# A transformer kernel: stage ends by halves of the tokens, the next stage opened with two natural weight units

## The chip, the cores and the metric

One core of one Trainium2 chip runs the whole program. The metric is the device time in microseconds (us); the median of three runs stands for a kernel. Engines are named as in the profile: PE is TensorE (matmuls, with its weight loads as PEld), DVE is VectorE, ACT is ScalarE, POOL is GpSimd, SP is SyncE, whose queue issues the loads of weights.

## The reference

Batch 1, 256 tokens, model width 1024, float32. Three blocks follow each other: a layer with mixer AB and a dense FFN, one with mixer CD and experts, and a second kind of block. The weight queue moves 475 MB:

```python
for layer in range(DEPTH):        # first_block: layer 0 and layer 1
    mix = _mixer_ab(x, ...) if layer % 2 == 0 else _mixer_cd(x, ...)
    x = _layernorm(ALPHA * x + mix, ln_g[layer, 0], ln_b[layer, 0])
    ffn = _swiglu(x, w1, w3, w2) if layer % 2 == 0 else _moe(x, w_router, w1, w3, w2)
    x = _layernorm(ALPHA * x + ffn, ln_g[layer, 1], ln_b[layer, 1])
# second_block
u = rms_norm(h, mix_norm_g); proj = u @ w_in     # block attention and a convolution
h = h + mixed @ w_out
u = rms_norm(h, ffn_norm_g)
h = h + (silu(u @ w_gate) * (u @ w_up)) @ w_down
return rms_norm(h, final_norm_g)
```

`_mixer_ab` holds gated linear attention and an attention over chosen keys, `_mixer_cd` an attention with forget gates (heads "c") and a dilated one (heads "d"), `_moe` the two best of eight experts.

## The kernel before

**Weights.** Each weight unit is 128 x 2048 float32 values (1 MB). SP loads units in the order in which they are used into a ring of six. Every product keeps float32 accuracy by three products of fp32r halves: ACT copies a unit's upper half (`upper`, line 1270), DVE subtracts it from the unit to give the lower half (`lower`, line 1697), and PE adds high x high, high x low and low x high (`thirds`, lines 611 to 614). There are two pairs of buffers for the halves (`Split.place`), a third one in the expert loop. `split_used` tells ACT that a pair is free, `taken` tells PE and SP that a unit is split. At the ends of stages POOL makes one lower half (its own `lower`, line 2302), at 18 and 18 + 33 units and at the second FFN's first unit.

**Tokens.** The 256 tokens are two tiles of 128 rows, tile 0 and tile 1, in `x[:, t, :]`. For the next stage they are transposed into `xTh` and `xTl`, the halves of x transposed, 8 blocks k of 128 model columns each.

**A stage's end.** The out units (or the last `down` units of an FFN) add up four banks, tile t and column half n in bank 4 + 2t + n. In the last unit, PE goes through (t, n) in the order 00, 01, 10, 11, and each finished bank raises `sums_part` or `sums_done`. DVE adds the residual (`residual_half`, line 1721); ACT computes mean and squared deviations of a tile (`deviations`, lines 1372 to 1374); POOL gives the reciprocal root (`rstd_tiles`, line 2293); DVE centres the tile (line 1756) and norms it by halves (line 1761; in the RMS norm line 1794), which raises `x_half` for tile 0 and `x_ready` for tile 1. PE's `transposes(src, n, spins=...)` (line 690) waits for these and writes banks 0 to 3; around it `keep_busy` issues matmuls on a constant tile (line 605), 16, 5 and 2 of them. ACT then copies four banks to `xTh` (line 1276) and DVE subtracts them to `xTl` (line 1707); `need(k)` in the first product of the next stage waits for `tr_low`.

**Where it happens.** A: end of mixer AB, next the dense FFN. B: end of the dense FFN, next mixer CD. C: end of mixer CD, next the router. D: end of the second block's mixer, next its FFN. The FFNs run chunks of 256 hidden columns: `up` multiplies two units with the weights stationary and both halves of x moving (512 columns, line 841, and 256 for the lower half, line 843), ACT and DVE compute the gate (`silus`, `gates`), and `down` adds the chunk to the sums. Mixer CD starts with `narrow` (forget logits, 8 columns, then a transposition by way of ACT), units in the order q, k, v for each pair of heads, and `cd_gap(i)`, which issues scores, turns and values of the 16 groups in the gaps between and in the middle of units, by hand-written lists (`CD_SCORES` and so on). The scores wait for `forget_low`, written by DVE (line 2051), and for the log-sigmoid (`ls_b`).

Each engine executes its own instruction stream in the order of the program, and they meet only through the semaphores named here.

## Time and profile before

| | |
|---|---|
| median of 3 runs | 1795.53 us (1792.7 to 1796.86) |
| the profiled execution | 1793.35 us, its span 1791.5 us |
| granted clock of PE, mean | 0.997 of 2.4 GHz |
| busy: PE, weight loads, DVE, ACT, POOL | 98%, 83%, 76%, 64%, 9% of the span |
| stages: AB, dense FFN, CD, router, experts, second mixer, second FFN | begin at about 0, 160, 354, 490, 512, 1449, 1591 us |

In the rows below, times are in us from the start of the span, a row's second number is the duration, and brackets hold the idle time of the engine before it and what ended it. `out<-in` names the tiles; for aliased buffers the name can be another tile's at the same place. The durations of matmuls in a row overlap, as PE is pipelined: what counts is the distance of their starts.

### The profile page before, as it was taken

Reading aid. Unit: us, or ns where it says so; the run is one execution under the profiler, and the core shown is the slowest. Engines: PE = TensorE matmul, PEld = TensorE weight load, DVE = VectorE, ACT = ScalarE, POOL = GpSimd, SP = SyncE. Lnnn points to the kernel's source line nnn. Section 1 sums busy time; section 2 is a strip of 40 time slices with the busy share of each in tenths; the row PEclk is TensorE's granted clock in tenths of the full one; section 3 lists DMA queues with packets and bytes.
Section 4 is the critical chain, followed back from the end, with each engine's and each line's share of the span. In section 5 each row is a group of like instructions: output and inputs, shape, how many; then the busy total and the mean of one; then the engine's idle time right before and its main releaser. Section 6 shows DMA issues by size and latency. Waiting matters only on the chain.

```text
span 1791.5 us, 24813 instructions
## 1 busy us (share of the span) xinstructions
PE 1762.9 (98%) x9332; PEld 1479.8 (83%) x9332; DVE 1353.4 (76%) x1280; ACT 1143.5 (64%) x1160; POOL 157.8 (9%) x107
## 2 busy tenths in 40 slices
PE   9999999999999999999999999999999999899998
PEld 7898888889878888888888888888888879878886
DVE  3765655545488888898888888988888888865555
ACT  5655545555467777777777777777777774555443
POOL 0002000100141000000000000000000105510000
PEclk9999999999999999999999999999999999999999
DMA  9845555543489999999999999999999986435550
GB/s 291 272 141 172 188 187 187 176 153 118 155 288 376 389 369 393 358 382 391 349 393 376 364 394 359 379 392 349 394 380 360 396 293 198 140 133 188 189 187 29
DMA packets 260196, 502.86 MB, mean 281 GB/s; under 512 B 15068, under 2 KB 101653, under 8 KB 259758
## 3 DMA queue, kind: packets, MB, share of 16 engines
q1 hardware_dynamic: 252160, 474.67, 74.0%
q0 software_dynamic: 7072, 26.69, 4.8%
q10 hardware_dynamic: 910, 0.76, 0.1%
q8 instruction: 36, 0.59, 0.1%
q14 instruction: 18, 0.15, 0.0%
HBM read 494.18 MB, written 12.65 MB: 283 GB/s over the span
## 4 chain that ended last, share of the span: by engine, by line
PE 89%; DVE 5%; ACT 2%; POOL 2%; DMA 1%; issue 1%; ACTq 0%; DVEq 0%; POOLq 0%; SPq 0%
PE psum L611 23%; PE psum L613 23%; PE psum L614 23%; PE psum L841 9%; PE psum L843 5%; DVE psum L2217 2%; PE psum L1126 1%; DMA ring<-in_w_in 1%; ACT wh L1270 1%; PE psum L750 1%; POOL wl L2302 1%; PE psum L718 1%; DVE x L1761 1%; POOL rstd L2293 1%; PE psum L734 0%
## 5 line engine op out<-in xcount | busy, mean ns | idle before, releaser
L1697 DVE TENSOR_TENSOR wl<-ring,wh 128x2048 fp32r<-128x2048 f32 x437 | 1001.4, 2292 | 248.0 <-ACT wh L1270 245.8
L1270 ACT ACTIVATE wh<-ring 128x2048 fp32r<-128x2048 f32 x450 | 862.3, 1916 | 271.2 <-PE psum L611 169.3
L611 PE MATMUL psum<-wh,xT 128*128 128x512 f32 (+1 forms) x1136 | 431.3, 380 | 1.4 <-DVE xT L1853 1.1
L614 PE MATMUL psum<-wh,xT 128*128 128x512 f32 (+1 forms) x1136 | 424.4, 374 | 0.0
L613 PE MATMUL psum<-wl,xT 128*128 128x512 f32 (+1 forms) x1136 | 424.3, 374 | 0.0
L611 PE MATMUL psum<-wh,wnh 128*128 128x512 f32 x672 | 266.3, 396 | 0.5 <-DVE wnl L1853 0.5
L614 PE MATMUL psum<-wh,wnl 128*128 128x512 f32 x672 | 263.5, 392 | 0.0
L613 PE MATMUL psum<-wl,wnh 128*128 128x512 f32 x672 | 263.5, 392 | 0.0
L841 PE MATMUL psum<-xT,wh 128*128 128x512 f32 x704 | 249.5, 399 | 0.4 <-DVE xT L1707 0.4
L611 PEld LDWEIGHTS psum<-wh,xT 128*128 128x128 f32 x1136 | 214.2, 189 | 43.0 <-issue 3.0
L614 PEld LDWEIGHTS psum<-wh,xT 128*128 128x128 f32 x1136 | 214.0, 188 | 39.8
L613 PEld LDWEIGHTS psum<-wl,xT 128*128 128x128 f32 x1136 | 214.3, 189 | 36.9
L843 PE MATMUL psum<-xT,wl 128*128 128x256 f32 x704 | 197.7, 281 | 0.0
L841 PEld LDWEIGHTS psum<-xT,wh 128*128 128x128 f32 x704 | 132.3, 188 | 33.9 <-issue 1.2
L611 PEld LDWEIGHTS psum<-wh,wnh 128*128 128x128 f32 x672 | 126.3, 188 | 28.4 <-issue 1.4
L614 PEld LDWEIGHTS psum<-wh,wnl 128*128 128x128 f32 x672 | 126.2, 188 | 28.4
L613 PEld LDWEIGHTS psum<-wl,wnh 128*128 128x128 f32 x672 | 126.3, 188 | 25.8
L843 PEld LDWEIGHTS psum<-xT,wl 128*128 128x128 f32 x704 | 132.9, 189 | 0.7
L611 PE MATMUL psum<-xT,wh 128*128 128x256 f32 x384 | 111.0, 289 | 1.9 <-DVE wl L1697 1.7
L613 PE MATMUL psum<-xT,wh 128*128 128x256 f32 x384 | 108.6, 283 | 0.0
L614 PE MATMUL psum<-xT,wl 128*128 128x256 f32 x384 | 108.5, 282 | 0.0
L611 PEld LDWEIGHTS psum<-xT,wh 128*128 128x128 f32 x384 | 73.4, 191 | 4.1 <-issue 3.0
(303 smaller groups left out, 1417.9 us busy)
## 6 DMA issues: line engine op xcount, KB each, us to landing
ring<-in_w_moe SPq DMA_DIRECT2D x336, 1024.0 KB, 6.8
ring<-in_w_dense SPq DMA_DIRECT2D x33, 1024.0 KB, 5.0
ring<-in_w_in_ab SPq DMA_DIRECT2D x14, 1024.0 KB, 10.9
ring<-in_w_in_cd SPq DMA_DIRECT2D x12, 1024.0 KB, 5.2
ring<-in_w_gate SPq DMA_DIRECT2D x11, 1024.0 KB, 5.1
ring<-in_w_up SPq DMA_DIRECT2D x11, 1024.0 KB, 5.2
ring<-in_w_down SPq DMA_DIRECT2D x11, 1024.0 KB, 4.8
ring<-in_w_in SPq DMA_DIRECT2D x6, 1024.0 KB, 8.2
```

Source lines behind the costliest of these rows:

```text
L611: last = pe.matmul(o, a[0], b_[0], start=first, stop=False)
L613: pe.matmul(o, a[0], b_[1], start=False, stop=False)
L614: return pe.matmul(o, a[1], b_[0], start=False, stop=final)
L718: last = pe.matmul(o, q[rows, hp, t * P:(t + 1) * P], k[rows, hp, 0:n], start=True, stop=not (forget or masked))
L750: last = pe.matmul(to[:, o:o + HD], pT[:, g % 2, (2 * hh + s) * P:(2 * hh + s + 1) * P], v[:, s, h * HD:(h + 1) * HD], start=(s == 0), sto ...
L841: first_of(pe.matmul(ps.rearrange("p (a t) -> p a t", a=2), h_[:, k, m], xT_both[:, :, k, :], start=k == 0, stop=False))
L843: last = pe.matmul(ps[:, 0:T], l_[:, k, m], xTh[:, k, :], start=False, stop=k == KT - 1)
L1126: last = pe.transpose(bank[2 + c % 2][:, f * P:(f + 1) * P], mg[:, f * P:(f + 1) * P], ident[:, :])
L1270: act.activation(upper_half[i], ring[:, u_, :], ACT.Copy).then_inc(hi_ready[s_], 1)
L1697: dve.tensor_tensor(lower_half[i], ring[:, u_, :], upper_half[i].bitcast(F32), ALU.subtract)\
L1761: dve.scalar_tensor_tensor(x[:, t, s_], src[:, t, s_], rstd[:, t:t + 1], w[:, 1, s_], ALU.mult, ALU.add).then_inc(x_ready if t else x_half, 1)
L2217: last = dve.scalar_tensor_tensor(summed(c, j), upad[:, c, j:j + T], cw[:, c, j:j + 1], summed(c, j - 1), ALU.mult, ALU.add)
```

## The change

- **Order of the sums.** `out_last` takes the place of the last two out units, `down_last` that of the last two `down` units: tile 0 of both units first, then tile 1.
- **Norms by tile.** `tile_norms` norms tile 0 by halves, its mean and variance from `bn_stats` on DVE; the residuals of tile 1 come behind the first half of tile 0. ACT still makes the deviations of tile 1 (`second_deviations`). `rms_norm` has the same order at D.
- **Pieces.** x is transposed in four pieces (tile, half of the k blocks), each copied and subtracted by itself (`turn_piece`, `copy_piece`, `lower_piece`). Not at C, where only the counts of spins change.
- **The pair.** `tile_pair` opens the dense FFN, mixer CD and the second FFN with two units in natural form (tokens stationary, 256 weight columns moving): the products with the upper weight halves piece by piece, then those with the lower halves. In the FFNs the pair is the first chunk's w1 and w3; its gate is computed in natural form on ACT and DVE (`silu_pair`, `gate_pair`) and transposed (`turn_hidden`); `first_up` takes the upper halves of the next unit first. In mixer CD the pair is the values of heads c, so q and k come after, and the lists of gaps move.
- **Buffers.** The third pair of halves, whose space is tq, nr, pr and pT, is used in the FFNs and for the units at their ends as well. POOL no longer makes lower halves at A, B and D; DVE makes them.

The diff, cut:

```diff
-CD_SCORES = [0, 1, 2, 3, 4, 5, 6, 7, 10, 11, 12, 13, 16, 17, 18, 19]
-CD_TURNED = [2, 3, 4, 5, 6, 7, 8, 9, 12, 13, 14, 15, 17, 18, 19, 20]
-CD_VALUES = [3, 4, 5, 6, 7, 8, 9, 10, 13, 14, 15, 16, 18, 19, 20, 21]
-CD_OUT_TURNED = [8, 14, 20, 22]
+CD_SCORES = [2, 3, 4, 5, 6, 7, 8, 9, 11, 12, 13, 14, 16, 17, 18, 19]
+CD_TURNED = [4, 5, 6, 7, 8, 9, 10, 11, 13, 14, 15, 15, 17, 18, 19, 20]
+CD_VALUES = [5, 6, 7, 8, 9, 10, 11, 12, 14, 15, 16, 16, 18, 19, 20, 21]
+CD_OUT_TURNED = [10, 15, 20, 22]
...
             AB["ra"], AB["ra"] + 256, AB["qb"] + 256, AB["kb"] + 256, AB["vb"] + 256]
-CD_ORDER = [CD[n + h] + 256 * i for h in "cd" for i in range(2) for n in "qkv"]
+CD_ORDER = [CD["vc"], CD["vc"] + 256] + [CD[n + "c"] + 256 * i for i in range(2) for n in "qk"] + \
+           [CD[n + "d"] + 256 * i for i in range(2) for n in "qkv"]
...
+                if self.s == 1 and n == 0:
+                    half = 2
+                elif n >= LENGTHS[0]:
+                    half = (LENGTHS[0] + 2 - n) % 3
+                elif after_out <= n < after_ffn:
+                    half = (n - 16) % 3 if self.s == 0 else (after_out + 2 - n) % 3
                 else:
-                    half = (n + 1) % 2
+                    half = n % 2
                 return ((n + N0[self.s]) % UNITS, self.rounds + (n // UNITS + 1), half, n + self.more)
...
+                n = self.n - 1
+                third = n < 54 if self.s == 0 else True
+                back = 2 if n > (18 if self.s == 0 else 11) and third or n >= LENGTHS[0] else 1
...
+            def turn_piece(src, n, t, kh):
+                pe.wait_ge(x_ready if t else x_half, 2 * n - 1 + kh)
+                for k in range(4):
+                    c = slice((4 * kh + k) * P, (4 * kh + k + 1) * P)
+                    last = pe.transpose(bank[2 * t + kh][:, k * P:(k + 1) * P], src[:, t, c], ident[:, :])
+                    first_of(last)
+                last.then_inc(tr_done, 1)
...
+            def tile_pair(src, n, done):
+                units = []
+                for j in range(2):
+                    u_, loads, i, at_ = halves.place()
+                    units.append([w.rearrange("p (k n) -> p k n", k=KT) for w in (upper_half[i], lower_half[i])]
+                                 + [u_, loads, at_])
+                turn_piece(src, n, 0, 0)
+                keep_busy(5, 3)
+                for i, (t, kh) in enumerate(PIECES):
+                    m = slice(t * P, (t + 1) * P)
+                    pe.wait_ge(tr_low, trs[0] + i + 1)
+                    for j, (h_, l_, u_, loads, at_) in enumerate(units):
+                        o = bank[4 + j][:, t * 256:(t + 1) * 256]
+                        if i == 0:
+                            pe.wait_ge(hi_ready[halves.s], at_ + 1)
+                        for k in range(4 * kh, 4 * kh + 4):
+                            pe.matmul(o, xTh[:, k, m], h_[:, k, :], start=t == 0 and k == 0, stop=False)
+                            pe.matmul(o, xTl[:, k, m], h_[:, k, :], start=False, stop=False)
+                        if j == 0 and i < 2:
+                            turn_piece(src, n, *PIECES[i + 1])
+                    if i == 1:
+                        turn_piece(src, n, *PIECES[3])
+                trs[0] += 4
+                for j, (h_, l_, u_, loads, at_) in enumerate(units):
+                    pe.wait_ge(taken[halves.s][u_], loads)
+                    for t in range(TT):
+                        m = slice(t * P, (t + 1) * P)
+                        for k in range(KT):
+                            last = pe.matmul(bank[4 + j][:, t * 256:(t + 1) * 256], xTh[:, k, m], l_[:, k, :],
+                                             start=False, stop=t == 1 and k == KT - 1)
+                            first_of(last)
+                    last.then_inc(done[j], 1)
+                    split_done()
...
+                def sums_of(j, w, t, ns):
+                    m = slice(t * P, (t + 1) * P)
+                    for n in ns:
+                        c = slice(n * 512, (n + 1) * 512)
+                        for kk in range(2):
+                            kx = 2 * j + kk
+                            last = thirds(bank[4 + 2 * t + n][:, :], (w[0][:, kk, c], w[1][:, kk, c]),
+                                          (xTh[:, kx, m], xTl[:, kx, m]), False, kx == KT - 1, turned=True)
+                        if j == 3:
+                            last.then_inc(sums_part if t + n < 2 else sums_done, 1)
+                two = split_unit("rows")
+                pe.wait_ge(o_low, turned)
+                sums_of(2, two, 0, (0, 1))
+                if gap is not None:
+                    gap()
+                sums_of(2, two, 1, (0,))
+                three = split_unit("rows")
+                pe.wait_ge(o_low, turned + 1)
+                sums_of(3, three, 0, (0, 1))
+                sums_of(2, two, 1, (1,))
+                split_done()
+                sums_of(3, three, 1, (0, 1))
+                split_done()
+                sums[0] += 1
...
                     for f in range(2):
                         ps = bank[2 * w + f]
...
+            def first_up(s):
+                u_, loads, i, at_ = halves.place()
+                h_, l_ = (w.rearrange("p (k n) -> p k n", k=KT) for w in (upper_half[i], lower_half[i]))
+                pe.wait_ge(hi_ready[s], at_ + 1)
+                for f in range(2):
+                    for k in range(KT):
+                        first_of(pe.matmul(bank[f].rearrange("p (a t) -> p a t", a=2), h_[:, k, f * P:(f + 1) * P],
+                                           xT_both[:, :, k, :], start=k == 0, stop=False))
+                pe.wait_ge(taken[s][u_], loads)
+                for f in range(2):
...
+                nine = split_unit("rows")
+                pe.wait_ge(h_low[s], 2 * 9 + 1)
+                sums_of(9, nine, 0, (0, 1))
+                sums_of(9, nine, 1, (0,))
+                ten = split_unit("rows")
+                pe.wait_ge(h_low[s], 2 * 10 + 1)
+                sums_of(10, ten, 0, (0, 1))
+                sums_of(9, nine, 1, (1,))
+                split_done()
...
+            def ffn(s, src, n):
+                def turn_hidden():
+                    pe.wait_ge(gated[s], 1)
+                    for f in range(2):
+                        for t in range(TT):
+                            last = pe.transpose(bank[6][:, f * T + t * P:f * T + (t + 1) * P],
+                                                mg[:, t * 256 + f * P:t * 256 + (f + 1) * P], ident[:, :])
+                            first_of(last)
+                    last.then_inc(up_done[s], 1)
+                tile_pair(src, n, (one_done[s], up_done[s]))
                 pe.wait_ge(sums_evac, sums[0])
-                up(s, 0)
-                up(s, 2)
-                down(s, 0, True, False)
+                first_up(s)
+                turn_hidden()
+                up(s, 2, sides=(1,))
+                down(s, 0, True)
...
-            for j in range(4):
-                out_unit(j, j + 1, (lambda: ab_gap(24 + 2 * j)) if j < 3 else None)
-                if j < 3:
-                    ab_gap(25 + 2 * j)
-            transposes(x, 1, spins=(16, 5, 2))
-            ffn(0)
-            transposes(x, 2, spins=(16, 5, 2))
+            for j in range(2):
+                out_unit(j, j + 1, lambda: ab_gap(24 + 2 * j))
+                ab_gap(25 + 2 * j)
+            out_last(3, lambda: ab_gap(28))
+            ffn(0, x, 1)
+            assert steps[0] == STEPS_PAIR
+            tile_pair(x, 2, (step_done, step_done))
+            steps[0] += 2
+            for i in range(2):
+                projected["v", CD_FIRST // 4 + i] = STEPS_PAIR + 1 + i
...
-            for w in range(12):
...
+            for w in range(2, 12):
+                middle = (lambda: cd_gap(2 * w - 6)) if w >= 4 else None
+                if w in (8, 11):
...
+            transposes(x, 3, spins=(5, 7, 2))
...
-            transposes(u, 6, spins=(12, 2, 2))
...
+            upper(a_pv, 8)
             upper()
-            deviations(0, y, u)
-            upper(sums_done, 1)
-            copy_transposed()
+            copy_piece(0, 0)
+            second_deviations(0)
+            for p in PIECES[1:]:
+                copy_piece(*p)
             ffn(0)
...
+                link(residual_half(0, 0, y, ALPHA, done, count))
+                dve.bn_stats(stat[:, 12:18], y[:, 0, 0:512])
+                residual_half(0, 1, y, ALPHA, done, count).then_inc(sums_ready, 1)
+                dve.wait_ge(sums_ready, 2 * n + 1)
+                link(dve.bn_stats(stat[:, 18:24], y[:, 0, 512:1024]))
+                link(dve.bn_aggr(mv[:, 0:2], stat[:, 12:24]))
+                first = ask_for(0, dve.tensor_scalar(e2[:, 0:1], mv[:, 1:2], LN_EPS, None, ALU.add))
+                norm_weights(n)
+                centred(0, 0, mv[:, 0:1])
+                dve.wait_ge(rs_got, first)
+                normed(0, 0)
+                residual_half(1, 0, y, ALPHA, done, count, stat[:, 4:5])
+                residual_half(1, 1, y, ALPHA, done, count, stat[:, 5:6]).then_inc(sums_ready, 1)
+                dve.wait_ge(sums_ready, 2 * n + 2)
+                dve.nop().then_inc(sums_evac, 1)
+                if by_piece:
+                    lower_piece(0, 0)
+                centred(0, 1, mv[:, 0:1])
+                normed(0, 1)
+                dve.wait_ge(dev_ready, 2 * n + 1)
+                centred(1, 0, stat[:, 6:7])
+                dve.wait_ge(dev_ready, 2 * n + 2)
+                second = ask_for(1, dve.tensor_scalar(e2[:, 1:2], ms[:, 1:2], 1.0 / D, LN_EPS, ALU.mult, ALU.add))
+                if by_piece:
+                    lower_piece(0, 1)
+                dve.wait_ge(rs_got, second)
+                normed(1, 0)
+                centred(1, 1, stat[:, 6:7])
+                normed(1, 1)
+                if by_piece:
+                    lower_piece(1, 0)
+                    lower_piece(1, 1)
+                dve.wait_ge(x_ready, 2 * norms[0])
+                dve.wait_ge(x_half, 2 * norms[0])
...
+                if n_sq == 1:
+                    summed(0, 0)
+                    summed(0, 1)
+                    mean_square(1, 0)
+                    norm_weights(n)
+                    dve.wait_ge(rs_got, squares_asked[2])
+                    dve.wait_ge(x2_ready, 2)
+                    scaled(0, 0)
+                    summed(1, 0)
+                    summed(1, 1)
+                    dve.wait_ge(x2_ready, 4)
+                    dve.nop().then_inc(sums_evac, 1)
+                    lower_piece(0, 0)
+                    scaled(0, 1)
+                    mean_square(1, 1)
+                    lower_piece(0, 1)
+                    dve.wait_ge(rs_got, squares_asked[3])
+                    scaled(1, 0)
+                    scaled(1, 1)
+                    lower_piece(1, 0)
+                    lower_piece(1, 1)
...
-            lower(0, 18)
...
-            lower(0, 18 + 3 * NCH_D)
...
-            lower(1, 11)
```

## Rows read from the trace of the kernel before

**Rows 1.** The page: busy time of each engine.

```profile
PE 1762.9 (98%) x9332; PEld 1479.8 (83%) x9332; DVE 1353.4 (76%) x1280; ACT 1143.5 (64%) x1160; POOL 157.8 (9%) x107
```

**Rows 2.** Windows at the four stage ends; busy time and count, clock, DMA.

```profile
159.80:168.70 8.90, 8.15 (x41) 5.67 (x39) 7.28 (x12) 5.20 (x10) 5.36 (x6) 1.00 0.38 119
353.60:362.40 8.80, 8.09 (x40) 5.61 (x39) 7.18 (x12) 5.12 (x10) 5.25 (x5) 1.00 0.38 119
489.90:498.50 8.60, 8.10 (x41) 5.66 (x40) 7.00 (x12) 5.15 (x10) 3.69 (x5) 1.00 0.08 27
1591.10:1598.20 7.10, 6.57 (x34) 4.38 (x32) 4.53 (x8) 4.37 (x9) 3.80 (x4) 1.00 0.45 148
```

**Rows 3.** Timeline of PE, end of mixer AB: start, duration, instruction.

```profile
159.61 0.40 PE L614 MATMUL psum<-wh,xT 128*128 128x512 f32 x1
159.84 3.81 PE L605 MATMUL psum<-spin 128*128 128x512 f32 x16
163.92 1.38 PE L690 MATMUL psum<-ident,x 128*128 128x128 f32 x8 [0.27 <-DVE x L1761]
165.05 1.41 PE L605 MATMUL psum<-spin 128*128 128x512 f32 x5
...
168.66 0.47 PE L841 MATMUL psum<-xT,wh 128*128 128x512 f32 x1 [0.25 <-DVE xT L1707]
...
169.09 0.40 PE L841 MATMUL psum<-xT,wh 128*128 128x512 f32 x1
...
169.80 0.40 PE L841 MATMUL psum<-xT,wh 128*128 128x512 f32 x1
```

**Rows 4.** Timelines of PE and DVE at the first scores of mixer CD.

```profile
389.56 0.46 PE L718 MATMUL psum<-tk,tq 64*128 64x128 f32 x3 [1.84 <-issue]
...
386.27 2.29 DVE L1697 TENSOR_TENSOR wl<-ring,wh 128x2048 fp32r<-128x2048 f32 x1 [3.48 <-ACT wh L1270]
```

**Rows 5.** Timeline of DVE, end of mixer AB.

```profile
160.04 0.69 DVE L1721 SCALAR_TENSOR_TENSOR y<-x,psum 128x512 f32<-128x512 f32 x1 [0.60 <-PE psum L614]
...
163.11 0.75 DVE L1761 SCALAR_TENSOR_TENSOR x<-y,rstd,lnw 128x512 f32<-128x512 f32 x1 [0.54 <-POOL rstd L2293]
...
167.83 2.48 DVE L1707 TENSOR_TENSOR xT<-psum,xT 128x512 fp32r<-128x512 f32 x4 [0.59 <-ACT xT L1276]
170.23 2.28 DVE L1697 TENSOR_TENSOR wl<-ring,wh 128x2048 fp32r<-128x2048 f32 x1
```

**Rows 6.** Timeline of POOL, end of mixer AB.

```profile
156.88 4.61 POOL L2302 TENSOR_TENSOR wl<-ring,wh 128x2048 fp32r<-128x2048 f32 x1 [6.13 <-ACT wh L1270]
161.46 1.54 POOL L2293 TENSOR_TENSOR rstd<-small,half 128x1 f32<-128x1 f32 x1
164.01 0.99 POOL L2293 TENSOR_TENSOR rstd<-small,half 128x1 f32<-128x1 f32 x1 [1.01 <-DVE small L1753]
```

**Rows 7.** Timeline of ACT, end of mixer AB.

```profile
167.10 2.07 ACT L1276 ACTIVATE xT<-psum 128x512 fp32r<-128x512 f32 x4 [2.72 <-PE psum L690]
```

**Rows 8.** Timeline of PE, first matmul of the last unit of the second FFN.

```profile
1777.47 0.47 PE L611 MATMUL psum<-wh,wnh 128*128 128x512 f32 x1
```

**Rows 9.** Timeline of DVE, statistics in the convolution's norm.

```profile
1569.64 0.69 DVE L2249 BATCH_NORM_STATS2 small<-psum 128x6 f32<-128x512 f32 x1
1570.36 0.18 DVE L2250 BATCH_NORM_AGGREGATE small<-small 128x2 f32<-128x6 f32 x1
```

**Rows 10.** Timeline of PE, two triples of a natural unit in mixer CD.

```profile
366.62 0.28 PE L611 MATMUL psum<-xT,wh 128*128 128x256 f32 x1
...
366.98 0.28 PE L611 MATMUL psum<-xT,wh 128*128 128x256 f32 x1
```

**Rows 11.** Windows near the start, and over the start of mixer CD.

```profile
8.00:10.00 2.00, 1.15 (x6) 0.27 (x4) 1.83 (x4) 1.60 (x4) 0.00 (x0) 1.00 1.10 348
12.00:14.00 2.00, 2.00 (x5) 0.54 (x4) 1.17 (x1) 1.53 (x3) 0.53 (x1) 0.52 0.51 51
362.00:390.00 28.00, 25.29 (x205) 23.23 (x204) 12.06 (x11) 14.37 (x19) 0.44 (x1) 1.00 0.50 152
```

317 lines of the change are left out of this document (206 added, 111 removed).

## The prediction

> **What bounds the kernel now.** I read first the page's busy times: TensorE (PE) is busy for 98% of the span [rows 1]. That figure hides the places I looked for next, because in the pauses between stages PE runs matmuls on a constant tile (`keep_busy`, line 605) whose results nobody reads. So the second view is the table of windows over the four places where a stage ends in a layer or RMS norm [rows 2]; in each of them PE is busy for over 90% of the window, at a granted clock of 1.00 (2.4 GHz). The third view is PE's timeline through the first of them, the end of mixer AB [rows 3]: the last useful matmul starts at 159.61, sixteen spins follow at 159.84, then transposes and more spins, and the next useful matmul starts at 168.66. That is 8.8 us without useful matmuls. I call the moment of the last useful matmul's end E (159.84 here). The same stretch is 8.8 us at the end of the dense FFN (B), 8.6 us at the end of mixer CD (C) and 7.0 us before the second FFN (D), the windows of [rows 2] less a tenth or so. Between these places PE waits next to nothing, with one exception: at 387.7 it waits 1.84 us for the first scores of mixer CD [rows 4], though the page calls the releaser "issue"; the code has `forget_low` there, which VectorE (DVE) writes behind a 2.29 us weight subtraction.
>
> What ends last in a stage end is a chain over DVE, POOL, ScalarE (ACT) and PE: residual (0.69 on DVE), reciprocal root on POOL (1.54, then 0.99), two halves of a norm (0.75 each), transposes, an ACT copy of 0.52 to 0.60 each and a DVE subtraction (0.62 each, one alone 0.68) [rows 5 to 7].
>
> **The change, part by part.** All times below are from E, at places A and B.
>
> *Out sums by tile (`out_last`, `down_last`).* The same 24 + 24 triples of matmuls are issued, no more. Spacing is 0.23 us (159.61 to 159.84 [rows 3]). Tile 0's two halves end 24 and 18 matmuls before the end, -5.5 and -4.1, where before they ended at -4.1 and -2.7. A cost: in `out_last` the wait for `o_low` of the last unit now stands 6 matmuls (1.4 us) behind the transposes of its input, where 12 covered it. The chain is 0.3 for PE's end, ACT 0.6, DVE 0.7, so 1.6: I put 0.25 at A and at C. `down_last` covers its last unit with 18 matmuls (4.1 us) where 24 did; that wait ended nearly in step with PE before (a matmul at 1777.47 with a start-up of 0.47 instead of 0.39 [rows 8]), and DVE does one weight subtraction fewer behind it (2.3 us earlier), so I put nothing, and 1.4 us as the upper bound at each FFN end.
>
> *Tile 0's norm before the end.* residual -5.25 to -4.55 (0.2 after its sums, as before); statistics of 0.69 (`bn_stats` of 512 columns [rows 9]), second residual, second statistics, aggregate 0.18 [rows 9] and a request of about as much: -1.95. POOL 1.54 [rows 6]: -0.35; it is no longer busy with a weight unit (4.61 us [rows 6]). Half a norm: 0.5. So PE can transpose piece (0,0) from 0.55. Four transposes take half of eight (163.92 to 165.05 [rows 3]), 0.56. Behind `normed(0,0)` on DVE stand both residuals of tile 1 (0.77 each with the accumulator): 2.0. The ACT copy ends at 2.0 too, the subtraction at 2.8, and PE has its first useful matmul at 2.85 instead of 8.8.
>
> *The pair (`tile_pair`).* It does the matmuls of two weight units as 96 of 256 columns at 0.12 (three in 0.36 [rows 10]), 11.5 us, where the FFN did 32 pairs of 512 and 256 columns at 0.355 (169.09 to 169.80 for two [rows 3]), 11.35. Per piece there are 1.9 us of upper-half work for both units. The DVE order sets the pieces: (0,1) needs half a norm in two operations (2.8 to 4.35), so PE waits 0.6 before its transposes; the subtraction of (0,1) ends at 6.55, PE waits 0.7. Then normed (1,0), centred and normed (1,1) end at 8.8, subtraction of (1,0) at 9.75 (PE waits 0.2), of (1,1) at 11.25 (no wait). The four pieces are done at 13.6. Only now are lower halves needed: DVE makes them at 11.25 to 13.55 and to 15.85 (2.28 each [rows 5]), so PE waits 0.4 before the second, and the pair ends at 17.8. Before, the two units ended at 8.8 + 11.35 = 20.15 in the FFN, and 8.8 + 11.5 = 20.3 in mixer CD. Gain 2.35 at A, 2.5 at B, before what follows.
>
> *Added behind the pair in the FFN.* The products are natural now, so `turn_hidden` adds 4 transposes, 0.56. `first_up` has the same columns as before in another order, nothing. The upper half of the third unit must be ready at 17.8; ACT is free at 10.5 and needs 1.9. ACT and DVE then reach the first `down` unit about when PE does (17.8 + 5.7 + 0.6 + 5.65, 29.7); I put 0.2. So A gives 2.35 - 0.56 - 0.2 - 0.25 = 1.3.
>
> *B, mixer CD.* Values come first, then the narrow products. DVE has four weight units before the log-sigmoid instead of three, but it is done with them 4.3 us behind the pair, and the log-sigmoid parts only arrive about 7.4 behind it; PE needs the result behind the q unit, at 9.5. So no new wait. The forget rows are then ready some 4 us before the first scores, which now stand one and a half units behind them instead of half a unit, and the 1.84 us wait [rows 4] goes. B gives 2.5 + 1.84 = 4.3. Nothing else in the reordered stage costs: the same 16 groups, each turn one or two half units behind its scores, as before.
>
> *C, router.* No pieces here. The transposes of tile 1 still wait for `normed(1,1)`, which is now at 7.6 or so behind three extra half operations; the first useful matmul comes at 8.4 to 8.6, as before. With the 0.25 of `out_last`: -0.2.
>
> *D.* The RMS norm asks POOL early, and a weight unit like the one of [rows 6] no longer stands ahead of the root. `scaled(0,0)` is ready before E, so the first useful matmul comes at 2.35: residual of (1,1) until 0.9, ACT copy until 1.5, subtraction until 2.3. The pair ends at 16.8 against 7.0 + 11.35 = 18.35. Less 0.56 and 0.2: 0.8.
>
> *The rest.* The third pair of split buffers, now used in the FFNs, lets ACT and DVE run a unit further ahead; PE is the bound there and has no pause to win back. The MoE loop (over half of the span) only changes the order in which buffers rotate: nothing. At the very end the last sums end where they did: nothing. SP issues the same loads in an order that follows the units; POOL's queue loses three subtractions and gets nothing.
>
> **Sum:** 1.3 + 4.3 - 0.2 + 0.8 = 6.2 us. The profiled execution took 1793.35 us, of which 1791.5 are the span; it becomes 1787.15. It lies 2.2 below the median of the runs, 1795.53, so the median becomes 1789.3. Bounds: if DVE's order costs nothing, pairs end at 16.05 instead of 17.8 (first matmul 2.85, 11.5 of work, three times 0.56), and 0.9 earlier at D: 4.4 more. Below: waits of 1.4 at both `down_last`, and each POOL root or DVE step a microsecond late in three places: 6 us less.
>
> *Two rules beside the rows.* The removed subtraction on POOL ran from 156.88 to 161.46 [rows 6], and DVE's residual in that time took 0.69 [rows 5], the duration that statistics of as many columns had with POOL idle [rows 9]. The Trainium skill, page "SBUF — State Buffer", section "SBUF: two separate sides", says that DVE and GpSimd lock a shared port pair for a whole instruction and the other fully blocks; by that rule the removal would also give DVE up to 4.6 us back at each of three places, and by the row it gives nothing, which is what my sum has.
>
> **Rivals.** (1) *DVE stays late* and the pieces arrive no sooner than the whole used to: for it speaks that everything now passes through one DVE queue that has taken POOL's 2.29 us units, and that a late root holds both residuals of tile 1 up behind it. If each pair loses 1.5 us, 4.5 of 6.2 are gone: 1793.8. (2) *DVE's order costs nothing*: 1784.9. (3) *The clock*, in two sizes. PE pauses for 0.6, 0.7, 0.2 and 0.4 us in each pair, and of the first 9 us behind E about 2.5 are idle, where spins filled them before. Near the start of this trace the clock fell: PE was busy for 1.15 of 2.00 us, and then the granted clock was 0.52, 1.2 GHz for most of the window, where 5 matmuls took 2.00 us, 0.40 each instead of 0.23 [rows 11]. A pair is busy for some 70%, between that 58% and the 92% of the old stage ends [rows 2], which kept 2.4 GHz. A short fall, some 4 us of 0.23 work at 0.40 to 0.46, costs 2 us; at three places it takes the gain: 1795.3. If instead the low clock holds through the four pieces, their 7.7 us of work take 7.7 more, less the 2 us of waits they then cover: 5.7 a pair, 17 in all, and the change is slower at 1806. It decides from a loss of 3.3 us a pair on. The Trainium skill, page "TensorE: Matmul & The Clock Gate", section "A second HAM failure mode: psum-queue depth-cycling", reports a kernel whose short pauses between groups of matmuls made the clock swing between its two levels; by that rule the larger size is what happens here. Against it speaks the start of mixer CD, whose window of 28 us has 2.7 without PE, the 1.84 us in one piece, at a granted clock of 1.00 [rows 11].
>
> **How the numbers follow.** A measurement of this kernel can tell about 0.2%, 3.6 us: faster is below 1791.9, slower above 1799.1. Forecast (1789.3, by itself 1786.5 to 1791.9) 0.52; DVE free (1784.9) 0.15; DVE late (1793.8) 0.18; short falls of the clock (1795.3) 0.07; long falls (1806) 0.08. Faster 0.67, same 0.25, slower 0.08. The range 1784 to 1796 takes in all but the long falls and some edges.
>
> **What would show it.** In the trace after: first useful matmul 2.9 us behind the last sum at A and B, 2.4 at D, 8.5 at C; end of the pair at 17.8 and 16.8; no 1.8 us wait before the first scores of CD; four more transposes in each FFN; clock 1.00 in the pairs. Wrong would be: the root arriving after E, waits over 1 us at the pieces or at `down_last`, a granted clock under 1.00 behind a stage end, or a new wait for `ls_b` in CD.

## The result and the profile after

The changed kernel takes 1781.41 us (median of 4 runs, 1780.12 to 1786.53) against 1794.15 (4 runs, 1792.70 to 1796.86). The ratio is 0.9925, with a 95% interval of 0.9906 to 0.9944: 10 to 17 us less, where 6.2 were forecast; the median lies below the forecast range. The profiled execution took 1781.14 us, 1779.3 of them the span, so 12.2 us less span than before. The ratios of the experiments below are taken against runs of the kernel before made beside each of them (medians 1795.3 to 1796.0 us).

The windows over the same four stage ends (columns: stretch, length, busy time and count of PE, weight load, DVE, ACT, POOL, then granted clock, DMA share, GB/s); compare [rows 2]:

```profile
159.80:168.70 8.90, 7.93 (x56) 6.71 (x56) 7.43 (x14) 3.77 (x8) 1.60 (x3) 1.00 0.00 1
349.50:358.40 8.90, 7.89 (x56) 6.69 (x56) 7.56 (x14) 3.66 (x8) 1.48 (x3) 1.00 0.00 0
1581.40:1588.50 7.10, 6.38 (x47) 5.58 (x46) 4.17 (x7) 2.71 (x7) 0.96 (x2) 1.00 0.00 0
```

PE is a little less busy here than before and yet ahead: its busy time is now mostly products that count, where [rows 2] counted spins. PE's timeline at the end of mixer AB, which answers to [rows 3]:

```profile
159.73 0.63 PE L736 MATMUL psum<-ident,x 128*128 128x128 f32 x4
160.11 1.42 PE L629 MATMUL psum<-spin 128*128 128x512 f32 x5
161.77 0.39 PE L757 MATMUL psum<-wh,xT 128*128 128x256 f32 x1 [0.24 <-DVE xT L1915]
...
163.22 0.66 PE L736 MATMUL psum<-ident,x 128*128 128x128 f32 x4 [0.24 <-DVE x L1986]
...
165.29 0.38 PE L757 MATMUL psum<-wh,xT 128*128 128x256 f32 x1 [0.46 <-DVE xT L1915]
...
172.26 4.07 PE L769 MATMUL psum<-wl,xT 128*128 128x256 f32 x32
176.16 3.82 PE L945 MATMUL psum<-xT,wh 128*128 128x512 f32 x16
...
181.73 0.60 PE L997 MATMUL psum<-ident,tk 128*128 128x128 f32 x4
```

E is 159.73. The first transposes start at E itself, the first useful product at E+2.04 (E+8.82 before), the lower halves of the weights at E+12.53, the unit behind the pair at E+16.43. Before, that unit started 32 matmul pairs behind the first useful product, at E+20.21:

```profile
180.05 0.40 PE L841 MATMUL psum<-xT,wh 128*128 128x512 f32 x1
```

B repeats the times of the changed kernel (351.59 and 365.97, E+2.04 and E+16.42); at D the first useful product comes at E+2.01. The scores of mixer CD [rows 4] have no wait any more:

```profile
385.47 0.49 PE L786 MATMUL psum<-tk,tq 64*128 64x128 f32 x4
```

Cut at the ends E of the four stages, which the timelines of both kernels give, the profiled executions compare as follows. The forecast's sum stands beside it, with each 0.25 for the wait in `out_last` put into the segment in which it falls.

| segment | before | after | gain | forecast |
|---|---|---|---|---|
| start to E at A | 159.84 | 159.73 | 0.11 | -0.25 |
| A to B | 193.78 | 189.82 | 3.96 | 1.55 |
| B to C | 136.28 | 131.03 | 5.25 | 4.05 |
| C to D | 1101.24 | 1100.86 | 0.38 | 0.05 |
| D to the last matmul | 191.63 | 189.12 | 2.51 | 0.8 |

The gains add up to 12.2. The experiments are compared by these segments too, since the first 20 us of a run differ between runs of one kernel by more than most of the terms (see the last section). The segment C to D has its own scatter: in three kernels below that do not differ from the changed one in this stretch (the GpSimd unit, no fillings, two deep) it read 1100.21, 1100.02 and 1100.39.

### The profile page after: what moved, and what is told of

It is laid out like the page before. It is cut to its first block, busy times and chain, and to the rows that moved or that the text cites. A ratio compares the mean times of both kernels' runs of the same rounds, so it can differ in the third digit from the quotient of the medians.

```text
span 1779.3 us, 24823 instructions
## 1 busy us (share of the span) xinstructions
PE 1747.7 (98%) x9348; PEld 1472.9 (83%) x9348; DVE 1362.0 (77%) x1280; ACT 1132.6 (64%) x1136; POOL 140.9 (8%) x104
## 4 chain that ended last, share of the span: by engine, by line
PE 90%; DVE 5%; ACT 2%; DMA 2%; issue 1%; POOL 1%; SPq 0%; POOLq 0%; DVEq 0%; ACTq 0%
PE psum L635 23%; PE psum L637 23%; PE psum L638 23%; PE psum L932 8%; PE psum L934 4%; DVE psum L2517 2%; PE psum L1271 1%; DMA ring<-in_w_in 1%; PE psum L818 1%; PE psum L786 1%; ACT wh L1413 1%; PE psum L769 1%; PE psum L757 1%; PE psum L758 1%; DMA ring<-in_w_in_ab 0%
## 5 line engine op out<-in xcount | busy, mean ns | idle before, releaser
L635 PE MATMUL psum<-wh,xT 128*128 128x512 f32 (+1 forms) x1104 | 421.2, 382 | 1.6 <-DVE xT L2124 1.1
L638 PE MATMUL psum<-wh,xT 128*128 128x512 f32 (+1 forms) x1104 | 415.4, 376 | 0.0
L637 PE MATMUL psum<-wl,xT 128*128 128x512 f32 (+1 forms) x1104 | 415.4, 376 | 0.0
L635 PEld LDWEIGHTS psum<-wh,xT 128*128 128x128 f32 x1104 | 208.1, 188 | 43.7 <-issue 4.1
L638 PEld LDWEIGHTS psum<-wh,xT 128*128 128x128 f32 x1104 | 207.7, 188 | 38.9
L637 PEld LDWEIGHTS psum<-wl,xT 128*128 128x128 f32 x1104 | 208.1, 189 | 37.0
L932 PE MATMUL psum<-xT,wh 128*128 128x512 f32 x608 | 215.7, 397 | 0.0
L934 PE MATMUL psum<-xT,wl 128*128 128x256 f32 x608 | 170.8, 281 | 0.0
L932 PEld LDWEIGHTS psum<-xT,wh 128*128 128x128 f32 x608 | 114.2, 188 | 27.9
L934 PEld LDWEIGHTS psum<-xT,wl 128*128 128x128 f32 x608 | 114.3, 188 | 0.7
L638 PE MATMUL psum<-xT,wl 128*128 128x256 f32 x384 | 108.4, 282 | 0.0
L635 PEld LDWEIGHTS psum<-xT,wh 128*128 128x128 f32 x384 | 73.4, 191 | 4.3 <-issue 3.3
```

The costliest lines, as they stand in the source:

```text
L635: last = pe.matmul(o, a[0], b_[0], start=first, stop=False)
L637: pe.matmul(o, a[0], b_[1], start=False, stop=False)
L638: return pe.matmul(o, a[1], b_[0], start=False, stop=final)
L932: first_of(pe.matmul(ps.rearrange("p (a t) -> p a t", a=2), h_[:, k, m], xT_both[:, :, k, :], start=k == 0, stop=False))
L934: last = pe.matmul(ps[:, 0:T], l_[:, k, m], xTh[:, k, :], start=False, stop=k == KT - 1)
```

## Experiments

The theory with which I went into them: GpSimd's root is not a fixed 1.54 us as [rows 6] seemed to say. It is 0.54 us of work, held up by whatever DVE operation with two inputs in SBUF runs beside it. The changed kernel runs a half-width centring (0.74) there instead of a full one, so the root takes 0.99, x is ready before E, and with that the whole pair comes earlier than forecast. DVE and POOL of the changed kernel at A:

```profile
157.62 0.74 DVE L1982 SCALAR_TENSOR_TENSOR x<-y,small,lnw 128x512 f32<-128x512 f32 x1
```

```profile
157.79 0.99 POOL L2592 TENSOR_TENSOR rstd<-small,half 128x1 f32<-128x1 f32 x1 [7.50 <-DVE small L1995]
...
164.10 0.55 POOL L2592 TENSOR_TENSOR rstd<-small,half 128x1 f32<-128x1 f32 x1 [5.32 <-DVE small L2011]
```

The first root ends at 158.78, 0.42 us behind the centring's end at 158.36; the second has DVE idle beside it and takes 0.55. The trace of the kernel before held two more signs, which the prediction did not use: [rows 6] have the same root at 1.54 and at 0.99, and DVE's centring of 1024 columns takes 1.56 at A, where it starts beside GpSimd's weight subtraction, but 1.28 at C, where none runs:

```profile
161.02 1.56 DVE L1756 SCALAR_TENSOR_TENSOR y<-y,small,lnw 128x1024 f32<-128x1024 f32 x1
...
491.10 1.28 DVE L1756 SCALAR_TENSOR_TENSOR y<-y,small,lnw 128x1024 f32<-128x1024 f32 x1
```

The rival: the root's length hangs on values or on how long GpSimd had been idle.

**The root alone.** DVE waits for the root and centres only then.

```diff
-                centred(0, 0, mv[:, 0:1])
                 dve.wait_ge(rs_got, first)
+                centred(0, 0, mv[:, 0:1])
                 normed(0, 0)
```

> The kernel after, with one operation moved: in the norm by tiles, centred(0, 0), which has two inputs in SBUF (y and the norm weights), stands behind the wait for POOL's root and not ahead of it, so VectorE is idle while POOL computes. Theory L (POOL's root and a VectorE operation with two SBUF inputs exclude each other: in both traces a root beside one ends 0.42 us behind its end): the first root of a layer norm takes 0.54 us in place of 0.99 at all three places A, B and C. Rival V (the root's length follows from its values or from how long POOL was idle): it stays at 0.99. The norm's first half then begins at most 0.4 us later, since the centring is now in series; both theories give about 1779 to 1781 us for the whole, so the duration decides.

Measured: 1781.19 us (one run). Same start against E, same values, same idle time of GpSimd, and 0.56 us:

```profile
157.63 0.56 POOL L2592 TENSOR_TENSOR rstd<-small,half 128x1 f32<-128x1 f32 x1 [7.50 <-DVE small L1995]
```

```profile
159.90 0.66 PE L736 MATMUL psum<-ident,x 128*128 128x128 f32 x4 [0.17 <-DVE x L1986]
```

The rival falls. What the root gains, the centring behind it takes back and a little more: E is 159.58 here, so the transposes start at E+0.32 (0.17 of it is the idle time in the row), and A to B takes 190.16 instead of 189.82.

**The GpSimd unit put back.** The lower halves of one weight unit at A and at B are computed by GpSimd again, as the kernel before did.

```diff
-            for _ in range(2):
-                lower()
+            halves.skip()
+            lower()
...
+            lower(0, 18)
...
+            lower(0, 18 + 3 * NCH_D)
```

> The kernel after, with the lower halves of the first unit of the pair at A and B given back to POOL, as before the change (one subtraction of 4.6 us each; VectorE does one of its units less). Theory L: the subtraction reads SBUF, so VectorE's centred(0, 0) cannot run beside it and shows up to 2 us in place of 0.74, the root stands behind the subtraction in POOL's queue, and the transposes of the first piece come 1.2 us later at each place: 2 to 3 us slower than the kernel after, some 1784. Without a lock (what I took in the prediction): centred(0, 0) stays at 0.74, only the queue delays the root, by 0.6 us each: 1 to 1.5 us slower. Third, if VectorE's work for weight units were the bound: faster than the kernel after.

Measured: 1783.95 us, ratio to before 0.9938 (0.9922 to 0.9955). DVE, then POOL, at A:

```profile
157.11 0.69 DVE L1928 SCALAR_TENSOR_TENSOR y<-x,psum 128x512 f32<-128x512 f32 x1
157.83 0.69 DVE L1993 BATCH_NORM_STATS2 small<-y 128x6 f32<-128x512 f32 x1
...
158.87 1.43 DVE L1982 SCALAR_TENSOR_TENSOR x<-y,small,lnw 128x512 f32<-128x512 f32 x1
160.83 0.75 DVE L1986 SCALAR_TENSOR_TENSOR x<-x,rstd,lnw 128x512 f32<-128x512 f32 x1 [0.53 <-POOL rstd L2593]
```

```profile
155.10 4.65 POOL L2602 TENSOR_TENSOR wl<-ring,wh 128x2048 fp32r<-128x2048 f32 x1 [3.55 <-ACT wh L1413]
159.72 1.00 POOL L2593 TENSOR_TENSOR rstd<-small,half 128x1 f32<-128x1 f32 x1
```

The residual reads PSUM and SBUF, the statistics read one operand: both take 0.69 beside GpSimd's subtraction, as with GpSimd idle. The centring reads two operands from SBUF and takes 1.43 instead of 0.74; it ends at 160.30, 0.55 behind the subtraction's end at 159.75, and the root ends 0.42 behind the centring. At B the centring took 1.62. The first transposes came 0.65 late at A and 0.84 at B, less than the 1.2 that the theory expected, and the transposes of `turn_hidden` at A 0.62 late: lateness of the first half of x goes through to the end of the pair nearly one to one. A to B grew by 0.62, B to C by 0.72. The median, 2.5 us above the changed kernel's, is near the theory's 1784.

**The centring of the kernel before, in halves.**

```diff
-                centred(0)
+                centred_half(0, 0)
                 dve.wait_ge(rs_got, asked[0])
                 normed(0, 0)
                 variance(1)
+                centred_half(0, 1)
                 normed(0, 1)
```

> The kernel before, with one edit: VectorE's centring of the first tile in the pair stages is done as two operations of 512 columns, the second after the root is used, in place of one of 1024. If GpSimd's root (one value per partition, 0.54 us when VectorE is idle) cannot read while VectorE runs an operation whose two inputs both lie in SBUF, and ends 0.42 us behind that operation, it takes 0.99 us in place of 1.54 in all three first roots (at 161.46, 355.21 and 492.0 of the trace of before), though it computes the same values and starts at the same point; the first half of the first tile is ready 0.5 us earlier, and the second half 0.2 later, so that the time moves by less than 1 us. If the root's length hangs on how long GpSimd had been idle or on its own operation ahead (the rival), it stays at 1.54.

Measured: 1796.61 us (one run), POOL at A:

```profile
162.50 0.99 POOL L2299 TENSOR_TENSOR rstd<-small,half 128x1 f32<-128x1 f32 x1
```

1.01 at B and 0.99 at C, where [rows 6] has 1.54: the theory's number in the old kernel. The time was missed: A to B is 0.19 longer, B to C 1.81. Of the latter 0.28 lie in the norm; the rest is a fall of the clock behind the wait for the scores, shown in the last section.

**All pieces first.** The pair transposes all four pieces, with fillings, before its first product.

```diff
+                for p in PIECES[1:]:
+                    turn_piece(src, n, *p)
+                    keep_busy(4, 7)
                 for i, (t, kh) in enumerate(PIECES):
-                    pe.wait_ge(tr_low, trs[0] + i + 1)
+                    if i == 0:
+                        pe.wait_ge(tr_low, trs[0] + 4)
...
-                        if j == 0 and i < 2:
-                            turn_piece(src, n, *PIECES[i + 1])
-                    if i == 1:
-                        turn_piece(src, n, *PIECES[3])
```

> The kernel after, where the pair starts its products only when all four pieces are transposed and split; all other orders as in it, with 4 spins between the pieces into another bank so that the clock has no reason to fall. It measures what the overlap of products and norm is worth. In the trace of after, the last piece is split 9.9 us behind the last sum; then 96 products of 0.12 us follow: the pair ends 21.5 behind it in place of 16.4, at three places: 15 us slower than the kernel after, near 1796, which is no better than before the change. If instead VectorE's queue were the bound within the pair (the rival of the prediction), the pieces would come earlier than 9.9 when nothing interrupts, and the loss would be 9 us or less.

Measured: 1796.00 us, ratio to before 1.0004 (0.9992 to 1.0015). At A, with E at 165.92:

```profile
169.40 0.66 PE L736 MATMUL psum<-ident,x 128*128 128x128 f32 x4 [1.70 <-DVE x L1986]
...
172.14 0.66 PE L736 MATMUL psum<-ident,x 128*128 128x128 f32 x4 [1.14 <-DVE x L1986]
...
175.66 0.38 PE L761 MATMUL psum<-wh,xT 128*128 128x256 f32 x1 [0.48 <-DVE xT L1915]
```

The first useful product comes at E+9.74. A to B is 4.84 longer than in the changed kernel, B to C 4.82, D to the end 4.40, 14.1 together, as expected: without the steps spread over the products the change is worth nothing. The rival, that DVE's queue is the bound within the pair, wanted the pieces clearly earlier once nothing interrupts, and a loss of 9 us or less; the last piece is split at E+9.68, only 0.3 earlier than in the changed kernel.

**The units in turn.** At a stage's end tile 1's sums of the last unit but one are no longer split around the last unit (the same in `down_last`).

```diff
-                sums_of(2, two, 1, (0,))
+                sums_of(2, two, 1, (0, 1))
+                split_done()
                 three = split_unit("rows")
...
-                sums_of(2, two, 1, (1,))
-                split_done()
```

> The kernel after, with the last two units of every out and down stage summed one after the other as before the change (the last unit still by tile). Tile 0's sums then end 2.7 us ahead of the end and not 4.1. In the trace of after, the first half of x is ready 0.1 us ahead of the last sum, so nearly all of the 1.4 us must show: the first useful matmul of A, B and D comes 1.2 to 1.4 us later (D has 0.8 us of slack, so 0.6 there), C about 1.0. In return the wait for the last turned input (0.3 us at A and C) goes. Sum: 3 to 4 us slower than the kernel after, some 1784.5. If the norm of tile 0 had slack everywhere: 0 to 1 us.

Measured: 1788.05 us, ratio 0.9950 (0.9930 to 0.9969). PE and DVE at A:

```profile
166.80 0.66 PE L736 MATMUL psum<-ident,x 128*128 128x128 f32 x4 [1.17 <-DVE x L1984]
```

```profile
161.59 0.69 DVE L1926 SCALAR_TENSOR_TENSOR y<-x,psum 128x512 f32<-128x512 f32 x1 [2.81 <-PE psum L638]
```

Tile 0's sums end six matmuls later, DVE starts 1.4 us later against E, and the transposes come 1.32 behind E at A and B and 0.7 at D, where no statistics are needed. At A and C the wait in `out_last` goes (0.35). From A to the last matmul the profiled execution is 3.5 us longer, inside the expected 3 to 4; the median is 6.6 above the changed kernel's, more than the stages explain, and in the profiled execution 5.8 us were lost ahead of A (see the last section). The chain ahead of E has no slack at A and B: it ends there within 0.1 us of E.

**No fillings.**

```diff
                 turn_piece(src, n, 0, 0)
-                keep_busy(5, 3)
```

> The changed kernel without the eight filling matmuls that run behind the first transposed piece of a pair (5 before the first product of the piece at 159.73 to 161.77 in its trace, 3 in their two smaller shapes). TensorE then stands still for 1.4 us more at the start of each of the three pairs, 2.0 us in one stretch. If the pairs are short because the pieces' steps are spread over the products (my theory), nothing moves: the first useful matmul still comes 2.04 us after the last product of the stage before, the granted clock stays at 1.00 (2.4 GHz) in the pair, and the time is that of the changed kernel within 0.5 us (1781 to 1782). If the clock is what the fillings buy (the rival), the granted clock falls to its lower level in the pair, its 256-column matmuls go from 0.12 us a piece to 0.21 for some us, and each of the three pairs costs 1.5 to 3 us: 1786 to 1790.

Measured: 1780.83 us, ratio 0.9912 (0.9893 to 0.9932). Windows at A, B (three) and D:

```profile
162.50:164.50 2.00, 0.69 (x6) 0.42 (x4) 1.84 (x6) 1.21 (x4) 0.00 (x0) 1.00 0.00 0
352.30:354.40 2.10, 0.70 (x6) 0.42 (x4) 1.93 (x6) 1.30 (x4) 0.00 (x0) 1.00 0.00 0
...
356.00:358.00 2.00, 2.00 (x11) 2.00 (x11) 1.10 (x3) 0.60 (x1) 0.54 (x1) 0.51 0.00 0
358.00:360.00 2.00, 2.00 (x13) 2.00 (x13) 1.97 (x4) 0.00 (x0) 0.00 (x0) 0.64 0.00 0
1584.20:1586.20 2.00, 0.69 (x6) 0.36 (x3) 1.33 (x3) 1.28 (x4) 0.00 (x0) 1.00 0.00 0
```

The first useful product comes at E+2.02 to E+2.04 as before. But my expectation of an untouched clock failed at one of three places: at B the granted clock fell to 0.51 (1.2 GHz) 1.6 us behind the pause, and B to C grew by 0.86; at A and D the same pause changed nothing. The rival, a fall in every pair, failed too. The three kernels at the end of this section have no fillings either; PE pauses there for 0.69 us at the same place, and all nine of their pairs stayed at 1.00.

**Later scores in the kernel before.** The first eight groups of scores, and what hangs on them, stand one place later.

```diff
-CD_SCORES = [0, 1, 2, 3, 4, 5, 6, 7, 10, 11, 12, 13, 16, 17, 18, 19]
+CD_SCORES = [1, 2, 3, 4, 5, 6, 7, 8, 10, 11, 12, 13, 16, 17, 18, 19]
```

> The kernel before, with one edit: in attention's second stage the first eight groups of scores stand one place later in the hand-written order, and the steps that hang on them (turned probabilities, values, first output piece) too. In the kernel before, the first group of scores waits 1.84 us for VectorE. If that wait is plain lateness of VectorE (my term B), the edit alone takes it away: TensorE's gap before the first scores goes from 1.84 us to under 0.3, and the end of that stage comes 1.3 to 1.9 us earlier, 1792.3 to 1793 in all against 1794.2. If the wait only moves (the rival: the chain behind the scores is the long one, and each group's steps then wait at a later place), the stage's end moves by under 0.5 us.

Measured: 1792.10 us, ratio 0.9985 (0.9974 to 0.9995).

```profile
393.03 0.49 PE L718 MATMUL psum<-tk,tq 64*128 64x128 f32 x4
```

No wait, and B to C takes 134.53 instead of 136.28: 1.75 of the 1.84. This term of the sum was right.

**Two buffers deep.** In the FFNs each split buffer is reused one unit earlier, as before the change.

```diff
+                first, end = (22, 18 + 3 * NCH_D) if self.s == 0 else (15, 11 + 3 * NCH_D)
+                if first <= n < end:
+                    return n - 1 + self.more
```

> The changed kernel, in which the weight halves of the two FFNs between their first and last units use each buffer again one unit earlier, as the kernel before did (two buffers deep, not three). If the third buffer is what took 0.03 us off each of the ten down units of an FFN (5.50 before, 5.47 after), they read 5.50 again and the time grows by 0.3 to 0.4 us per FFN, 0.6 to 0.8 in all: the segment from the first stage's end to the second's grows from 189.82 us to 190.15, and the last one alike. If the units are shorter for another reason (the order of the matmuls, the other lines), the units stay at 5.47 and both segments stay within 0.1 us.

Measured: 1788.38 us, ratio 0.9955 (0.9937 to 0.9972). Both theories missed. The down units stay at 5.46 us, so the third buffer is not what shortens them. But at the end of each FFN PE stands still; PE, then the windows:

```profile
345.36 0.39 PE L641 MATMUL psum<-wh,wnl 128*128 128x512 f32 x1
348.06 0.47 PE L638 MATMUL psum<-wh,wnh 128*128 128x512 f32 x1 [2.31 <-DVE wnl L2173]
```

```profile
348.00:350.00 2.00, 1.95 (x6) 1.56 (x7) 0.00 (x0) 1.26 (x1) 0.00 (x0) 0.73 1.04 352
350.00:352.00 2.00, 2.00 (x6) 1.63 (x5) 1.38 (x2) 0.00 (x0) 0.00 (x0) 0.50 0.44 146
```

DVE's last gated products wait behind a weight subtraction that had to wait for its buffer. That costs 2.47 us, and at B a fall of the clock behind it 1.8 more: A to B grew by 4.23, D to the end by 2.61 (2.47 of wait, clock 1.00). The forecast had the third buffer at nothing; with `down_last` as it is, it is what keeps the 1.4 us bound that I had put there from coming true.

**The router's unit on VectorE.** In the changed kernel DVE's small operation and PE's next products in the router stage:

```profile
492.79 0.93 DVE L2378 TENSOR_TENSOR small<-small 128x2 f32<-128x2 f32 x1
```

```profile
494.87 0.28 PE L1215 MATMUL psum<-small,cum 128*128 128x8 f32 x1 [0.74 <-DVE small L2382]
```

The edit, in the code of DVE and of POOL:

```diff
-            halves.skip()
             tile_norms(sums_done, 2, False)
...
+            lower()
...
-            lower(0, LENGTHS[0])
```

> The changed kernel, in which the lower half of the router stage's first weight unit is computed by VectorE, behind its own transposed lower halves, and no longer by GpSimd (whose subtraction runs from 489.08 to 493.70 in the changed kernel's trace). Theory of the shared port: VectorE's operation of 2 values per partition took 0.93 us there because it reads SBUF twice and waits for the end of GpSimd's subtraction; without that subtraction it takes under 0.3, the TensorE gap of 0.74 us ahead of the router's last products shrinks to 0.4 or less, and the time falls by 0.3 to 0.7 us (1780.7 to 1781.1). The rival: VectorE's own subtraction of the unit, 2.29 us, comes to stand ahead of the norm it must do next, and the stage grows by up to 2 us.

Measured: 1780.79 us, ratio 0.9923 (0.9902 to 0.9943).

```profile
492.47 0.16 DVE L2378 TENSOR_TENSOR small<-small 128x2 f32<-128x2 f32 x1
```

Two values per partition: 0.16 us instead of 0.93, and the PE wait of 0.74 is gone. (In the kernel before, the end of GpSimd's subtraction fell on this operation too: 0.56 us.) The experts start at E+20.81 instead of E+21.58, 0.77 earlier. The time itself can't tell 0.8 us from scatter; the timeline can.

**Upper products first.** Of each piece, the products with its upper part are issued behind ACT's copy, those with its lower part behind DVE's subtraction; no fillings.

```diff
-                    pe.wait_ge(tr_low, trs[0] + i + 1)
+                    pe.wait_ge(tr_evac, trs[0] + i + 1)
...
-                            pe.matmul(o, xTl[:, k, m], h_[:, k, :], start=False, stop=False)
+                        if j == 0 and i == 2:
+                            turn_piece(src, n, *PIECES[3])
+                    pe.wait_ge(tr_low, trs[0] + i + 1)
+                    for j, (h_, l_, u_, loads, at_) in enumerate(units):
+                        for k in range(4 * kh, 4 * kh + 4):
+                            pe.matmul(bank[4 + j][:, t * 256:(t + 1) * 256], xTl[:, k, m], h_[:, k, :],
+                                      start=False, stop=False)
```

> The changed kernel with another order inside the pair of natural units: of each transposed piece the products with its upper part are issued first, for both units, as soon as ScalarE's copy is there, and the products with its lower part only behind VectorE's subtraction; the next piece is transposed behind the first unit's lower products, the last piece behind the third's first upper products; the filling matmuls go. If the first useful product waits for the chain transpose, copy, subtraction (0.60, 0.60 and 0.69 us), it comes 0.7 us earlier, E+1.3 in place of E+2.04 (E is the end of the last product of the stage before), and the waits of 0.46 and 0.27 us inside the pair go too, so that each of the first two pairs ends 0.7 to 1.0 us earlier and the third (at 1583.45) 0.7: 2 to 2.7 us in all, 1778.7 to 1779.4. If VectorE's own row of work sets the pair's end (the rival: the second piece needs the normed half at 163.16 whatever TensorE does), the first product comes earlier and the second piece's wait grows by as much: under 0.5 us in all.

Measured: 1783.94 us, ratio 0.9939 (0.9923 to 0.9955). PE, then DVE, with E at 159.60:

```profile
160.91 1.21 PE L755 MATMUL psum<-wh,xT 128*128 128x256 f32 x8 [0.69 <-ACT xT L1435]
...
172.04 1.22 PE L772 MATMUL psum<-wl,xT 128*128 128x256 f32 x8 [0.30 <-DVE wl L1901]
```

```profile
169.70 4.48 DVE L1901 TENSOR_TENSOR wl<-ring,wh 128x2048 fp32r<-128x2048 f32 x2
```

The first useful product comes at E+1.31, 0.73 earlier as expected, and nothing of it is left at the end (A to B 190.04, B to C 131.22, D to the end 189.10). The expected gain of 2 to 2.7 us did not come: A to B, B to C and D to the end are together 0.4 us longer than in the changed kernel. Part of the rival is right, VectorE's row sets the end, but at another place than it said: the lower half of the first weight unit, which DVE starts only behind its last piece.

**Both.** 

> Both edits of the two kernels before it (the router stage's unit on VectorE, and the upper products first). They touch different stages, so their gains should add within 0.3 us: 1778.0 to 1779.0 by the theories, 1781 to 1783 by the rivals.

Measured: 1782.03 us, ratio 0.9921 (0.9906 to 0.9937), in the rivals' range, since only one of the two edits had a gain to add. C to D is 1099.27 against 1100.19 without the router edit; the pairs are as in the kernel above.

**The lower half between the last two pieces.** Both edits, and:

```diff
                     lower_piece(1, 0)
+                    lower()
                     lower_piece(1, 1)
```

> The kernel with both edits (upper products first, router unit on VectorE), and one more: in each of the three pairs VectorE computes the lower half of the first natural unit between its last two transposed lower halves, where it idled 1.2 us, and no longer behind the last. In the run with the upper products first the lower-half products waited for exactly this subtraction (0.30 us at 1592.78, 0.46 us of gap before 172.04), though all pieces were done. If VectorE's place of that subtraction is what now sets the pair's end, the wait goes to the last piece's lower products instead and shrinks: each pair ends 0.4 to 0.9 us earlier than in the kernel without this edit, 1.2 to 2.7 us over the three, and against the changed kernel the whole is 2 to 3.5 us shorter: 1778 to 1779.5. If the last piece's lower products now wait as long for their own subtraction, which comes 1.0 us later (the rival), the pairs end where they did within 0.2 us each.

Measured: 1779.26 us (6 runs, 1777.86 to 1784.85), ratio to before 0.9911 (0.9896 to 0.9925). DVE at D:

```profile
1592.67 2.28 DVE L1901 TENSOR_TENSOR wl<-ring,wh 128x2048 fp32r<-128x2048 f32 x1
1594.87 0.68 DVE L1918 TENSOR_TENSOR xT<-psum,xT 128x512 fp32r<-128x512 f32 x1
```

The segments are 189.45, 130.63, 1099.23 and 188.48, so each pair ends 0.6 us earlier than with the upper products first and 0.4 to 0.6 earlier than in the changed kernel. The first was expected at 0.4 to 0.9. From A to the last matmul it is 3.0 us shorter than the changed kernel, 0.8 of this by the router and 0.9 in the experts' stretch, where nothing was edited. It is the best of the kernels by the timelines; its interval and that of the changed kernel overlap, so the times alone don't show it.

## Why the prediction was wrong in size

The direction, the places and the mechanism came out, twice as large. Of the 6.0 us beyond the forecast's 6.2 about 3.6 lie in the three pairs, whose end the sum put too late. By its steps:

- **Tile 0's norm before the end.** Failed step: "POOL 1.54 [rows 6]". Measured 0.99, 1.00 at B, and the piece can be transposed at E and not at 0.55. The 1.54 holds only beside a centring of 1024 columns. This is 0.55 of the 1.4 us by which a pair ended earlier than forecast. The root alone (0.56), the halves in the kernel before (0.99 to 1.01) and the unit put back (1.43 for the centring) show it; that lateness here goes through to the pair's end is shown by the last of them (0.65 in, 0.62 out) and by the first (0.32 in, 0.34 out). I had the rule in hand. The Trainium skill, page "SBUF — State Buffer", section "SBUF: two separate sides", limits the lock on DVE's side to a two-port mode or an operation with two SBUF inputs. I set it aside because of a residual that took 0.69 beside GpSimd, and a residual reads one of its inputs from PSUM: that row could not test the rule. A row that could was the centring of the kernel before, 1.56 beside the subtraction against 1.28. The runs here agree with the page: the operations with two inputs in SBUF were held up (0.74 became 1.43, 0.16 became 0.93), those with one were not (0.69 both ways).
- **The pair.** Failed term: its end at 17.8; measured 16.43. Besides the 0.55 of the root, four transposes take 0.38 (159.73 to 160.11), not 0.56 (I had halved the 1.13 of eight in [rows 3], where the second four probably waited for their half of x); residuals with their accumulator start 0.61 apart (159.56 and 160.17), where I took 0.77. So the second piece is transposed at 3.49 and not at 4.35. The upper halves' work is done at 12.53 instead of 13.6, and the 0.4 of waiting for a lower half did not occur. That is 1.4 us at A and at B and the same steps at D. I had this case among the bounds ("DVE's order costs nothing", 16.05), and as a rival at 1784.9 with 0.15.
- **Behind the pair.** `turn_hidden` takes 0.36 (181.73 to 182.09), not 0.56; the 0.2 for the first `down` unit is nothing. No term had the `down` units: each takes 5.47 instead of 5.50 us, about 0.3 per FFN, and the last two of the first FFN 10.91 instead of 11.13 (338.64 to 349.55 after, 342.49 to 353.62 before), partly because the short wait with its start-up, as in [rows 8], is gone. Why the others are shorter stays open: it isn't the third buffer. With the pair's 1.4 these make up the 2.4 us by which A to B beat the forecast.
- **B.** The scores' 1.84 was right (1.75 in the kernel before alone). The rest of the segment's surplus is the pair.
- **C.** First useful product at E+7.56 instead of 8.4 to 8.6, 1.0 earlier than before. The gain shrank to 0.6 by the experts' start, since GpSimd's subtraction now falls wholly on DVE's small operation (0.93, before 0.56), shown by the router edit. The wait in `out_last` was right: 0.28 seen and 0.08 of start-up behind it, 0.25 forecast.
- **D.** Forecast 0.8, measured 2.51: the pair's 0.9 (it ends at E+15.95, not 16.8), 0.2 each for the transposes and the first `down` unit, 0.4 for the other down units.
- **Clock.** No pair of the changed kernel fell below 1.00, though PE pauses up to 0.46 us in it. The run without fillings shows that the rival had a true core (one of its three pairs fell to 0.51); that the fillings are what holds it off is not shown. The Trainium skill, page "TensorE: Matmul & The Clock Gate", section "A second HAM failure mode: psum-queue depth-cycling", reports a clock that swings under such short pauses between groups of matmuls; in these pairs, with pauses up to 0.46 us, it did not.
- **DVE stays late.** Not seen as a rival of the whole, but the run with the upper products first shows that, once the first product comes earlier, DVE's row is what ends last in a pair.

## What to carry to other kernels

A duration read beside other work is not the price of the operation: before it goes into a sum, look which operands that work and its neighbours read, and find the same operation once with its neighbour idle. A rule may only be set aside by a row that meets the rule's conditions. When a step ahead of a long chain is made earlier, follow the next operation of every engine behind it; here 0.73 us at the front bought nothing until one subtraction in VectorE's queue was moved as well.
